# Regrouping a convolution tile and moving its layer norm between attention rounds in a two-block float32 forward pass

## The chip, the cores and the metric

The kernel runs on one core of a Trainium2 chip. The metric is device time in microseconds (us) of one execution of the whole program, as the median of several runs; lower is better. Five engines work side by side, each through its own instruction list in order, and they meet only at semaphores: TensorE (PE in the profile, with its weight loads as PEld), VectorE (DVE), ScalarE (ACT), GpSimd (POOL) and SyncE (SP), which here only issues transfers.

## The reference, cut to what matters

Two transformer blocks run one after the other on 512 tokens of width 1024. The change touches the middle of the second block only, which is this (`B, S = 1, 512`, eight heads of 64, 512 convolution channels, 31 taps):

```python
def _conformer_conv(val, gate, conv_w, conv_b, ln_g, ln_b):
    glu = val * jax.nn.sigmoid(gate)
    padded = jnp.pad(glu, ((0, 0), (CONV_WIDTH - 1, 0), (0, 0)))
    y = depthwise_conv(padded, conv_w) + conv_b            # 31 taps, 512 channels
    return jax.nn.silu(_layernorm(y, ln_g, ln_b))          # over the 512 channels

def second_block(...):
    u = _rmsnorm(h, g_pre_mix) @ w_in                      # val, gate, q, k, v
    conv_out = _conformer_conv(c_val, c_gate, conv_w, conv_b, conv_ln_g, conv_ln_b)
    # A[t,s] = sigmoid(z_ts) * prod_{s<j<t} (1 - sigmoid(z_tj)), s < t, per head
    attn_out = _rmsnorm(_stick_breaking(q, k, v), attn_norm_g)     # norm over each head's 64
    y = concat([conv_out, attn_out]) @ w_out               # the output product
    h = h + _rmsnorm(y, g_post_mix)
    # then a gated feed-forward part of width 2816 and a last residual
```

## The kernel before, in words

Every float32 product is made of three TensorE matmuls (`mm3`, lines 745 to 747): operands are split into a high part (fp32r) and a rest, and high by high, high by low and low by high are summed. Weights come in slabs of 128 x 1024; ScalarE makes the high part (`weights`, line 1375), VectorE the low part (line 1853).

The second block keeps channels on the partitions and the 512 tokens along the free axis. Channels 0 to 383 of the convolution (tiles 0 to 2) are done tap by tap on VectorE (`taps`, line 2264, 93 taps in all). Tile 3 is done on TensorE into PSUM bank 7: each tap is a product with a diagonal 128 x 128 matrix, whose high and low parts (`DH`, `DL`, 16 places) GpSimd makes in one instruction each for a run of taps (line 721). `CV_GROUPS` says which taps form a group; a group is one accumulation in bank 7, and its result is then copied or added into `CV[:, 3]` (`co`).

`PLAN_C` is a hand-written list of steps that all four engines walk in the same order; each engine issues only its part of a step. It has eight rounds, one for each head `u`:

- `lg u`: logits on TensorE (line 1158 and `mm3`), then Abs, Exp and Ln on ScalarE (lines 1706, 1708, 1710)
- `sp u`, `sl u`: softplus on VectorE (line 2314), its split (ScalarE line 1715, VectorE line 2318)
- `bt u-1`: the suffix sums on TensorE (line 1173); `ex u-1`: Exp of them (line 1721); `ah`/`at`: the split of the weights (lines 1727, 2322)
- `va u-2`: the product with the values, into bank 6; `kp`: its copy, and for odd heads the square (lines 1733, 1737)
- `ps`, `pr`, `pt`, `pl`: the norm of a pair of heads: sums by TensorE (line 1226) with a first VectorE step (line 1859), rsqrt and copy (line 1745), transposes into bank 7 (line 1231) with the multiplication (line 2337), and the split into the output product's input `M2h`/`M2l` (lines 1751, 2341)
- one step of `BEHIND`: in rounds 0 to 3 an input tile (q2, k2, q3, k3), in rounds 4 to 6 a convolution group, in round 7 the layer norm's sums `ln_sub`

The layer norm of the convolution is: `ln_sub` (sum over channels on TensorE, line 1239; subtraction on VectorE, line 2345; squares on ScalarE, line 1757), `ln_var` (sums of the squares, 32 matmuls of two columns, line 1245), `ln_rs` (rsqrt), `ln_mul` (transposes, line 1251; multiplication, line 2354), then for each tile `silu` (lines 1763, 1766) and `ll` (line 2358).

After the eight rounds stands a tail with the last heads, the rest of the norms and the first strips of the output product. `OUT_KS` says which two 128-row parts of the mixed input a slab of `w_out` covers: rows 0 to 3 are the convolution tiles, rows 4 to 7 the head pairs. `OUT` is the order of the eight slabs (column half n, slab j); a slab is four strips (128 tokens each) of six matmuls into bank 4n + t. Banks 0 to 2 and 3 to 5 carry the logits of even and odd heads, bank 6 the values, bank 7 everything in `IN_7`, each of whose steps waits until the one before has been read.

Of the kernel before, what the change touches and what calls it, by code (L numbers as in the profile page):

```python
# [98 lines left out]
def build(nc, cols, ins, out):  # L99
    sems = {}  # L100

    def S(name):
        if name not in sems:
            sems[name] = nc.alloc_semaphore(f"s_{name}")
        return sems[name]
# [63 lines left out]
    SL, CH = {}, {}  # L169
# [62 lines left out]
    for x in IN_LATER:  # L232
        in_tile(x)

    OUT_KS = [[4, 5], [6, 7], [0, 1], [2, 3]]
    OUT = [(0, 0), (0, 1), (0, 2), (1, 0), (1, 1), (1, 2), (0, 3), (1, 3)]
    for n, j in OUT:
        SL["out", n, j] = slab([(W["w_out_2"][0], 512 * n, 512)], 128 * OUT_KS[j][0], 2)
# [136 lines left out]

    CV_GROUPS = [range(0, 10), range(10, 20), range(20, 31)]
    TAPS = [(j, k) for j in range(3) for k in range(31)]
    PLAN_C = []  # L380
    for n, x in enumerate(IN_FIRST):
# [1 line left out]
    for j in range(4):  # L383
        PLAN_C += [("v2", j), ("w", CH["v2"].first + min(j, 2) + 3), ("taps", 4)]
    PLAN_C += [("v2_out",)]
    BEHIND = [("tile", x) for x in IN_LATER] + [("cv", g) for g in range(3)] + [("ln_sub",)]
    for u in range(8):
        b = BEHIND[u - 1] if u else ("", "")
        if b[0] == "tile":
            PLAN_C += [("ev", b[1])]  # L390
        elif b[0] == "cv":
            PLAN_C += [("co", b[1])]
        PLAN_C += [("lg", u), ("taps", 2)]
        if u >= 4:
            PLAN_C += [("pt" if u % 2 else "ps", u // 2 - 2)]
        PLAN_C += [("taps", 2)]
        if u >= 1:
            PLAN_C += [("bt", u - 1)]
        if u >= 2:
            PLAN_C += [("va", u - 2)]  # L400
        PLAN_C += [("sp", u)]
        if u >= 1:
            PLAN_C += [("ex", u - 1)]
        if b[0] == "tile":
            PLAN_C += [("lo", b[1])]
        if u >= 4 and u % 2 == 0:
            PLAN_C += [("pr", u // 2 - 2)]
        PLAN_C += [("sl", u)]
        if u >= 1:
            PLAN_C += [("ah", u - 1), ("at", u - 1)]  # L410
        if u >= 2:
            PLAN_C += [("kp", u - 2)]
        PLAN_C += [BEHIND[u]]
        if u < 5:
            PLAN_C += [("w", CH["v2"].last + min(u, 3) + 4)]
        if u >= 4 and u % 2:
            PLAN_C += [("pl", u // 2 - 2)]
        PLAN_C += [("taps", 2 if u < 6 else 100)]
    PLAN_C += [("bt", 7), ("ps", 2), ("va", 6), ("ex", 7), ("pr", 2), ("o", (0, 1, 2)), ("ah", 7), ("at", 7), ("kp", 6),
               ("ln_var",), ("pt", 2), ("ln_rs",), ("va", 7), ("kp", 7), ("pl", 2), ("ps", 3), ("pr", 3), ("ln_mul",),  # L420
               ("o", (3,)), ("pt", 3), ("silu", 0), ("pl", 3)]
    for j in range(1, 4):
        PLAN_C += [("silu", j), ("ll", j - 1)]
    PLAN_C += [("ll", 3)]

    PAIR_SUMS = {4: 1, 2: 0, 6: 2}
    EV = [s[1] for s in PLAN_C if s[0] == "tile" and s[1][0] != "v"]
# [214 lines left out]
    def gpsimd_program(e):  # L642
# [59 lines left out]
        for step in PLAN_C:  # L702
            if step[0] == "tile" and step[1][0] == "g":
                j = GATES.index(step[1])
                q.wait_ge(S("sig"), j + 1)
                TTT(T4[:, j % 2, :], T4[:, j % 2, :], RB[:, :], ALU.mult).then_inc(S("sig_r"), 1)
            elif step[0] == "cv":

                taps = CV_GROUPS[step[1]]
                for part in ([k for k in taps if k < 16], [k for k in taps if k >= 16]):  # L710
                    if not part:
                        continue
                    n, k0 = len(part), part[0] % 16
                    q.wait_ge(S("w_used"), SL["in", "k3"] + 1)
                    q.wait_ge(S("cw"), 2)
                    if part[0] >= 16:
                        q.wait_ge(S("cv_used"), 1 + (part[-1] >= 26))
                    eye = IDENT.unsqueeze(1).broadcast_to([128, n, 128])
                    at = slice(part[0], part[-1] + 1)
                    for dst, w in ((DH, CWH[:, at].bitcast(F32)), (DL, CWL[:, at])):  # L720
                        TTT(dst[:, k0:k0 + n, :], eye, w.unsqueeze(2).broadcast_to([128, n, 128]), ALU.mult).then_inc(
                            S("diag"), 1)
# [9 lines left out]
    def tensor_program(e):  # L732
# [456 lines left out]
        def conv_group(g):  # L1189
            taps = CV_GROUPS[g]  # L1190
            q.wait_ge(S("cv_g"), 1)
            for k in taps:
                q.wait_ge(S("diag"), 8 if g == 2 else 6 if k >= 16 else 2 * g + 2)
                x = slice(k, k + T)
                m = mm3(banks[7][:, :], DH[:, k % 16, :], DL[:, k % 16, :], GLH[:, x], GLL[:, x], k == taps[0],
                        k == taps[-1])
            m.then_inc(S("cv_used"), 1)

        def block_step(kind, *a):
            step = (kind,) + a  # L1200
            if step in IN_7:
                free_7(step)
            if kind == "tile":
                n = IN_FIRST.index(a[0]) if a[0] in IN_FIRST else -1
                tile_t(Ah, Al, "pre_mix", n % 4 if n >= 0 else 7, lambda: in_free(n) if n >= 0 else None,
                       turn_in_tile(X, "pre_mix") if n == 0 else no_step)
                if n == 0:
                    q.wait_ge(S("turn_lo"), 8 * JOB["pre_mix"] + 8)
                    spread(X, "pre_mix")
            elif kind == "v2":  # L1210
                v2_slab(a[0])
            elif kind == "lg":
                logits(a[0])
            elif kind == "bt":
                between(a[0])
            elif kind == "va":
                values(a[0])
            elif kind == "cv":
                conv_group(a[0])
            elif kind == "o":  # L1220
                out_first(a[0])
            elif kind == "ps":
                q.wait_ge(S("pair_sq"), a[0] + 1)
                q.wait_ge(S("keep"), 2 * a[0] + 2)
                for t in range(4):
                    m = mm(banks[6][:, 2 * t:2 * t + 2], OQ[:, 128 * t:128 * t + 128], HALF[:, :], start=True, stop=True)
                m.then_inc(S("pair_ps"), 1)
            elif kind == "pt":
                q.wait_ge(S("pair_b"), a[0] + 1)
                for t in range(4):  # L1230
                    m = e.transpose(banks[7][:, 128 * t:128 * t + 128], TN[:, 128 * t:128 * t + 128], IDENT)
                m.then_inc(S("pair_t"), 1)
            elif kind == "ln_sub":
                for j in range(4):
                    if j == 3:
                        q.wait_ge(S("cv_ev"), len(CV_GROUPS))
                    else:
                        q.wait_ge(S("tap"), 31 * j + 31)
                    m = mm(banks[7][:, :], ONES, CV[:, j, :], start=j == 0, stop=j == 3)
                m.then_inc(S("ln_ps"), 1)  # L1240
            elif kind == "ln_var":
                for t in range(4):
                    for j in range(4):
                        q.wait_ge(S("ln_act"), j + 1)
                        m = mm(banks[7][:, 2 * t:2 * t + 2], GL[:, j, 128 * t:128 * t + 128], ONES[:, 0:2], start=j == 0,
                               stop=j == 3)
                m.then_inc(S("ln_ps"), 1)
            elif kind == "ln_mul":
                q.wait_ge(S("rs_n"), 3 * USE["ln",] + 3)
                for t in range(4):  # L1250
                    m = e.transpose(banks[7][:, 128 * t:128 * t + 128], LNR[:, t:t + 1].broadcast_to([128, 128]), IDENT)
                m.then_inc(S("ln_ps"), 1)
# [18 lines left out]
        def out_strip(w, j, n, t):  # L1271
            return strip(w, OUT_KS[j], t, 4 * n + t, M2h, M2l, mixed_ready, j == 0, j == 3)

        def out_first(tiles):
# [4 lines left out]
            for t in tiles:  # L1279
                q.wait_ge(S("sb_exp"), 21 if t < 3 else 24)  # L1280
                m = out_strip(held, 0, 0, t)
                if t == 3:
                    m.then_inc(S("w_used"), 1)

        def last_strips(order, step, done):

            w = []
# [10 lines left out]
        held.clear()  # L1298
        for step in PLAN_C:
            block_step(*step)  # L1300
        q.wait_ge(S("pair_n"), 4)
        q.wait_ge(S("keep"), 8)
        for n, j in OUT[1:5]:
            w = next_slab()
            for t in range(4):
                m = out_strip(w, j, n, t)
            m.then_inc(S("w_used"), 1)
        last_strips(OUT[5:], out_strip, "o_tile")


# [47 lines left out]
    def scalar_program(e):  # L1358
# [316 lines left out]
        def block_step(kind, *a):  # L1675
# [71 lines left out]
            elif kind == "pl":  # L1747
# [1 line left out]
                q.wait_ge(S("pair_n"), p + 1)  # L1749
                q.wait_ge(S("w_used"), SL["in", "k3"] + 1)  # L1750
                act(M2h[:, 4 + p, :], TN, ACT.Copy).then_inc(S("pair_hi"), 1)
            elif kind == "ln_sub":
                q.wait_ge(S("tap"), len(TAPS))
                q.wait_ge(S("cv_g"), 1)
                for j in range(4):
# [81 lines left out]
    def vector_program(e):  # L1837
# [450 lines left out]
        def block_step(kind, *a):  # L2288
# [49 lines left out]
            elif kind == "pl":  # L2338
                p = a[0]
                q.wait_ge(S("pair_hi"), p + 1)  # L2340
                tt(M2l[:, 4 + p, :], TN, M2h[:, 4 + p, :].bitcast(F32), ALU.subtract).then_inc(S("pair_lo"), 1)
            elif kind == "ln_sub":
                q.wait_ge(S("ln_ps"), 1)
                for j in range(4):
                    stt(CV[:, j, :], banks[7][:, :], -1.0 / 512, CV[:, j, :], ALU.mult, ALU.add).then_inc(S("ln_dve"), 1)
# [153 lines left out]
```

## Time and profile before

| what | value |
|---|---|
| median of 3 runs | 1868.67 us (1867.34 to 1868.72) |
| the profiled execution's own time | 1870.3 us |
| span of its trace (first to last instruction) | 1868.5 us |
| mean granted TensorE clock | 0.986 |
| PE busy | 1812.6 us, 97% |
| DVE, ACT, POOL busy | 953.3, 751.7, 127.4 us |
| chain that ended last | PE 86%, DVE 10%, ACT 3% |

A time "in the trace" is counted from the first instruction of the span. In the timeline view, instructions of one line that follow each other are merged into a row with their count; a bracket at the end of a row is how long the engine stood idle before it and which instruction released it. The stretch that the change touches lies between 1350 and 1487 us.

### The profile page before, as it was taken

Reading aid. Unit: us, or ns where it says so; the run is one execution under the profiler, and the core shown is the slowest. Engines: PE = TensorE matmul, PEld = TensorE weight load, DVE = VectorE, ACT = ScalarE, POOL = GpSimd, SP = SyncE. Lnnn points to the kernel's source line nnn. Section 1 sums busy time; section 2 is a strip of 40 time slices with the busy share of each in tenths; the row PEclk is TensorE's granted clock in tenths of the full one; section 3 lists DMA queues with packets and bytes.
Section 4 is the critical chain, followed back from the end, with each engine's and each line's share of the span. In section 5 each row is a group of like instructions: output and inputs, shape, how many; then the busy total and the mean of one; then the engine's idle time right before and its main releaser. Section 6 shows DMA issues by size and latency. Waiting matters only on the chain.

```text
span 1868.5 us, 21601 instructions
## 1 busy us (share of the span) xinstructions
PE 1812.6 (97%) x8477; PEld 1482.4 (79%) x8477; DVE 953.3 (51%) x1702; ACT 751.7 (40%) x1475; POOL 127.4 (7%) x163
## 2 busy tenths in 40 slices
PE   8999999999999999999999999998998999999997
PEld 7887888888887777777888888786777788888886
DVE  5666443434345666755344434489954544243345
ACT  7333432323235565644232323423765543232233
POOL 0000010101001111001010101010020000000000
PEclk9999999999999999999999999999998999999999
DMA  7222233333332111112333333232100333333331
GB/s 246 81 69 90 72 109 90 102 94 99 101 95 80 57 57 57 35 57 81 100 99 95 98 95 99 79 91 68 46 11 1 91 101 102 100 92 102 91 101 56
DMA packets 195748, 158.37 MB, mean 85 GB/s; under 512 B 5248, under 2 KB 161152, under 8 KB 195648
## 3 DMA queue, kind: packets, MB, share of 16 engines
q1 hardware_dynamic: 194240, 154.16, 27.4%
q0 software_dynamic: 400, 1.25, 0.3%
q8 instruction: 67, 1.10, 0.2%
q10 hardware_dynamic: 1008, 1.59, 0.2%
q14 instruction: 33, 0.27, 0.0%
HBM read 154.88 MB, written 2.10 MB: 84 GB/s over the span
## 4 chain that ended last, share of the span: by engine, by line
PE 86%; DVE 10%; ACT 3%; issue 1%; DMA 0%; SPq 0%; DVEq 0%; ACTq 0%
PE ps L745 28%; PE ps L747 27%; PE ps L746 27%; DVE sb L2264 3%; DVE sb L1853 1%; PE ps L797 1%; PE ps L1173 1%; PE ps L1061 0%; DVE sb L2388 0%; DVE sb L1879 0%; PE ps L1067 0%; DVE sb L1851 0%; PE ps L856 0%; PE ps L1037 0%; DMA sb<-in_mem 0%
## 5 line engine op out<-in xcount | busy, mean ns | idle before, releaser
L745 PE MATMUL ps<-sb,sb 128*128 128x512 f32 (+3 forms) x2547 | 991.1, 391 | 16.9 <-DVE sb L1859 5.5
L747 PE MATMUL ps<-sb,sb 128*128 128x512 f32 (+3 forms) x2547 | 968.2, 382 | 0.0
L746 PE MATMUL ps<-sb,sb 128*128 128x512 f32 (+3 forms) x2547 | 968.1, 382 | 0.0
L745 PEld LDWEIGHTS ps<-sb,sb 128*128 128x128 f32 (+1 forms) x2547 | 479.8, 189 | 125.8 <-issue 19.7
L747 PEld LDWEIGHTS ps<-sb,sb 128*128 128x128 f32 (+1 forms) x2547 | 479.5, 189 | 93.0
L746 PEld LDWEIGHTS ps<-sb,sb 128*128 128x128 f32 (+1 forms) x2547 | 480.6, 190 | 86.0
L1853 DVE TENSOR_TENSOR sb<-sb,sb 128x512 fp32r<-128x512 f32 x532 | 351.4, 700 | 347.2 <-ACT sb L1375 346.3
L1375 ACT ACTIVATE sb<-sb 128x512 fp32r<-128x512 f32 x532 | 305.5, 622 | 428.4 <-PE ps L747 427.1
L2068 DVE TENSOR_TENSOR sb<-sb,sb 128x512 fp32r<-128x512 f32 x64 | 68.0, 1063 | 176.9 <-ACT sb L1524 176.9
L1534 ACT ACTIVATE sb<-ps 128x512 f32<-128x512 f32 x64 | 38.4, 599 | 208.6 <-PE ps L747 208.6
L651 POOL TENSOR_TENSOR sb<-sb 128x512 f32<-128x512 f32 x64 | 66.9, 1045 | 786.6 <-ACT sb L1534 786.6
L2264 DVE SCALAR_TENSOR_TENSOR sb<-sb,sb,sb 128x512 f32<-128x512 f32 x90 | 74.0, 823 | 2.4
L2048 DVE SCALAR_TENSOR_TENSOR sb<-ps,sb,sb 128x512 f32<-128x512 f32 x64 | 47.9, 749 | 18.9 <-PE ps L747 18.3
L2431 DVE TENSOR_TENSOR sb<-ps,sb 128x512 f32<-128x512 f32 x22 | 15.2, 692 | 72.1 <-PE ps L747 71.6
L1810 ACT ACTIVATE sb<-sb 128x512 f32<-128x512 f32 x22 | 13.9, 633 | 93.8 <-DVE sb L2431 93.8
L797 PE MATMUL ps<-sb,sb 128*128 128x128 f32 x176 | 28.2, 299 | 15.0 <-DVE sb L1879 5.4
L1524 ACT ACTIVATE sb<-sb 128x512 fp32r<-128x512 f32 x64 | 39.9, 624 | 5.1 <-POOL sb L651 5.1
L1879 DVE SCALAR_TENSOR_TENSOR sb<-ps,sb,sb 128x512 fp32r<-128x512 f32 (+1 forms) x48 | 31.4, 701 | 18.9 <-ACT sb L1394 18.9
L2438 DVE TENSOR_TENSOR sb<-ps,sb 128x512 f32<-128x512 f32 x22 | 15.2, 692 | 48.0 <-PE ps L747 48.0
L797 PEld LDWEIGHTS ps<-sb,sb 128*128 128x128 f32 x176 | 22.5, 152 | 20.9 <-DMA sb<-in_con 5.2
L1851 DVE SCALAR_TENSOR_TENSOR sb<-sb,sb,sb 128x512 fp32r<-128x512 f32 x40 | 29.5, 748 | 17.8 <-ACT sb L1375 17.6
L1394 ACT ACTIVATE sb<-ps,sb 128x512 fp32r<-128x512 f32 (+1 forms) x48 | 28.5, 656 | 11.8 <-PE ps L797 11.7
(203 smaller groups left out, 1000.8 us busy)
## 6 DMA issues: line engine op xcount, KB each, us to landing
sb<-in_w_up SPq DMA_DIRECT2D x86, 512.0 KB, 4.0
sb<-in_w_down SPq DMA_DIRECT2D x86, 512.0 KB, 3.8
sb<-in_w_gate SPq DMA_DIRECT2D x22, 512.0 KB, 3.8
sb<-in_a_w_in SPq DMA_DIRECT2D x20, 512.0 KB, 3.9
sb<-in_w_in SPq DMA_DIRECT2D x20, 512.0 KB, 3.7
sb<-in_w_o SPq DMA_DIRECT2D x16, 512.0 KB, 3.8
sb<-in_w_mem_kv SPq DMA_DIRECT2D x8, 512.0 KB, 7.7
sb<-in_w_out SPq DMA_DIRECT2D x8, 512.0 KB, 3.8
```

What stands on the lines that cost most here:

```text
L651: TTT(T2[:, z, :], T1[:, z, :], T1[:, z, :], ALU.mult).then_inc(S("relu2"), 1)
L745: mm(ps, lh, rh, start=start, stop=False, **k)
L746: mm(ps, lh, rl, start=False, stop=False, **k)
L747: return mm(ps, ll, rh, start=False, stop=stop, **k)
L797: i = e.transpose(banks[4 + k % 4][:, 128 * t:128 * t + 128], src[:, t, 128 * k:128 * k + 128], IDENT)
L1375: act(WH[i % N_SPLIT][:, a], RAW[i % N_RAW][:, a], ACT.Copy, scale=g).then_inc(S("w_hi"), 1)
L1524: act(Bh[:, m % 8, :], T2[:, m % 2, :], ACT.Copy).then_inc(S("h_hi"), 1)
L1534: act(T1[:, m % 2, :], banks[m % 4][:, :], ACT.Relu).then_inc(S("relu"), 1)
L1853: tt(lo, raw, hi, ALU.subtract).then_inc(S("w_lo"), 1)
L2048: stt(x, ps, rms2(job, t, 1), x, ALU.mult, ALU.add).then_inc(S("res"), 1)
L2068: tt(Bl[:, m % 8, :], T2[:, m % 2, :], Bh[:, m % 8, :].bitcast(F32), ALU.subtract).then_inc(S("h_lo"), 1)
L2264: stt(CV[:, j, :], GL[:, j, k:k + T], col("convw", 4 * k + j), CV[:, j, :], ALU.mult, ALU.add).then_inc(S("tap"), 1)
```

## The change

Three things, all in the second block. The convolution tile on TensorE is done in two groups of 16 and 15 taps in place of three of 10, 10 and 11, so that its layer norm's `ln_sub` stands in round 6 instead of round 7; the subtraction (`ln_dv`, VectorE) and the squares (`ln_sq`, ScalarE) become steps of their own in round 7. The tail begins with `ln_var`, ahead of `bt 7`, and `ln_mul` and the `silu` steps come ahead of the third pair's norm. The rows of the output product are taken as 4-5, 0-1, 2-3, 6-7, and two slabs, (0,1) and (0,2), are multiplied (`os`) between the steps of the last pair's norm; the wait for the last pair's norm and for the last `kp` stands only where banks 6 and 7 are needed.

```diff
-    OUT_KS = [[4, 5], [6, 7], [0, 1], [2, 3]]
+    OUT_KS = [[4, 5], [0, 1], [2, 3], [6, 7]]
...
-    CV_GROUPS = [range(0, 10), range(10, 20), range(20, 31)]
+    CV_GROUPS = [range(0, 16), range(16, 31)]
...
-    BEHIND = [("tile", x) for x in IN_LATER] + [("cv", g) for g in range(3)] + [("ln_sub",)]
+    BEHIND = [("tile", x) for x in IN_LATER] + [("cv", g) for g in range(2)] + [("ln_sub",), ("none",)]
...
         PLAN_C += [("lg", u), ("taps", 2)]
+        if u == 7:
+            PLAN_C += [("ln_dv",)]
         if u >= 4:
             PLAN_C += [("pt" if u % 2 else "ps", u // 2 - 2)]
...
             PLAN_C += [("ah", u - 1), ("at", u - 1)]
+        if u == 7:
+            PLAN_C += [("ln_sq",)]
         if u >= 2:
             PLAN_C += [("kp", u - 2)]
...
-    PLAN_C += [("bt", 7), ("ps", 2), ("va", 6), ("ex", 7), ("pr", 2), ("o", (0, 1, 2)), ("ah", 7), ("at", 7), ("kp", 6),
-               ("ln_var",), ("pt", 2), ("ln_rs",), ("va", 7), ("kp", 7), ("pl", 2), ("ps", 3), ("pr", 3), ("ln_mul",),
-               ("o", (3,)), ("pt", 3), ("silu", 0), ("pl", 3)]
+    PLAN_C += [("ln_var",), ("bt", 7), ("ps", 2), ("ln_rs",), ("va", 6), ("ex", 7), ("pr", 2), ("o", (0, 1, 2)), ("ah", 7),
+               ("at", 7), ("kp", 6), ("ln_mul",), ("va", 7), ("silu", 0)]
     for j in range(1, 4):
         PLAN_C += [("silu", j), ("ll", j - 1)]
-    PLAN_C += [("ll", 3)]
+    PLAN_C += [("pt", 2), ("ll", 3), ("pl", 2), ("o", (3,)), ("kp", 7), ("w", SL["out", 0, 0] + 4), ("os", 0, 1), ("ps", 3),
+               ("pr", 3), ("w", SL["out", 0, 0] + 5), ("os", 0, 2), ("pt", 3), ("pl", 3)]
...
-                        q.wait_ge(S("cv_used"), 1 + (part[-1] >= 26))
+                        q.wait_ge(S("cv_used"), 1)
...
-                q.wait_ge(S("diag"), 8 if g == 2 else 6 if k >= 16 else 2 * g + 2)
+                q.wait_ge(S("diag"), 2 * g + 2)
...
+        def out_slab(n, j):
+            w = next_slab()
+            for t in range(4):
+                if (n, t) == (1, 2):
+
+                    q.wait_ge(S("pair_n"), 4)
+                    q.wait_ge(S("keep"), 8)
+                m = out_strip(w, j, n, t)
+            m.then_inc(S("w_used"), 1)
...
-        q.wait_ge(S("pair_n"), 4)
-        q.wait_ge(S("keep"), 8)
-        for n, j in OUT[1:5]:
-            w = next_slab()
-            for t in range(4):
-                m = out_strip(w, j, n, t)
-            m.then_inc(S("w_used"), 1)
+        for n, j in OUT[3:5]:
+            out_slab(n, j)
         last_strips(OUT[5:], out_strip, "o_tile")
```

## Rows read from the trace of the kernel before

**Rows 1.** The page: engine totals; the chain that ended last, by engine.
```profile
PE 1812.6 (97%) x8477; PEld 1482.4 (79%) x8477; DVE 953.3 (51%) x1702; ACT 751.7 (40%) x1475; POOL 127.4 (7%) x163
...
PE 86%; DVE 10%; ACT 3%; issue 1%; DMA 0%; SPq 0%; DVEq 0%; ACTq 0%
```

**Rows 2.** Timeline of PE, 1360 to 1424 us: start, length, what.
```profile
1360.88 0.76 PE L745 MATMUL ps<-sb,sb 128*128 128x512 f32 x1 [3.34 <-DVE sb L1859]
...
1372.62 0.50 PE L745 MATMUL ps<-sb,sb 64*128 64x512 f32 x1
...
1376.29 3.06 PE L1173 MATMUL ps<-sb,sb 128*128 128x256 f32 x20
1379.19 0.40 PE L745 MATMUL ps<-sb,sb 128*128 128x512 f32 x1
...
1381.14 0.40 PE L745 MATMUL ps<-sb,sb 128*128 128x512 f32 x1
...
1388.20 0.50 PE L745 MATMUL ps<-sb,sb 64*128 64x512 f32 x1
...
1404.99 0.49 PE L745 MATMUL ps<-sb,sb 64*128 64x512 f32 x1
...
1413.51 3.60 PE L1239 MATMUL ps<-sb,sb 128*128 128x512 f32 x8
...
1416.54 3.39 PE L1173 MATMUL ps<-sb,sb 128*128 128x256 f32 x20
...
1422.84 0.48 PE L745 MATMUL ps<-sb,sb 128*128 128x512 f32 x1 [2.13 <-DVE sb L1859]
```

**Rows 3.** Timeline of DVE in round 4: a tap beside GpSimd, one alone.
```profile
1353.30 2.81 DVE L2264 SCALAR_TENSOR_TENSOR sb<-sb,sb,sb 128x512 f32<-128x512 f32 x1
...
1360.58 0.16 DVE L1859 TENSOR_SCALAR sb<-ps 128x8 f32<-128x8 f32 x1
1360.69 0.75 DVE L2264 SCALAR_TENSOR_TENSOR sb<-sb,sb,sb 128x512 f32<-128x512 f32 x1
```

**Rows 4.** Timeline of POOL: the first diagonal instruction alone, and the first four.
```profile
1350.48 2.34 POOL L721 TENSOR_TENSOR sb<-sb,sb 128x1280 fp32r<-128x1280 f32 x1 [101.56 <-PE ps L747]
...
1350.48 8.84 POOL L721 TENSOR_TENSOR sb<-sb,sb 128x1280 fp32r<-128x1280 f32 x4 [101.56 <-PE ps L747]
```

**Rows 5.** Windows: busy us (count) of PE, PEld, DVE, ACT, POOL; clock; DMA.
```profile
1361.00:1367.00 6.00, 6.00 (x19) 5.18 (x20) 3.97 (x9) 2.99 (x4) 0.00 (x0) 0.52 0.00 0
...
1446.00:1451.00 5.00, 4.62 (x11) 3.38 (x12) 3.01 (x5) 4.54 (x7) 0.00 (x0) 0.50 0.00 0
```

**Rows 6.** Timelines of DVE and ACT: rounds 6 and 7.
```profile
1401.42 1.62 DVE L2322 TENSOR_TENSOR sb<-sb,sb 128x1408 fp32r<-128x1408 f32 x1
...
1418.24 2.48 DVE L2345 SCALAR_TENSOR_TENSOR sb<-ps,sb 128x512 f32<-128x512 f32 x4
...
1411.84 1.45 ACT L1721 ACTIVATE sb<-ps 128x512 f32<-128x512 f32 x3
1413.75 1.38 ACT L1715 ACTIVATE sb<-sb 128x1408 fp32r<-128x1408 f32 x1 [0.46 <-DVE sb L2314]
...
1419.04 2.34 ACT L1757 ACTIVATE sb<-sb 128x512 f32<-128x512 f32 x4 [1.36 <-DVE sb L2345]
```

**Rows 7.** Timeline of PE: the tail (1245 twice: up to 1431.6, and whole).
```profile
1428.98 2.92 PE L1245 MATMUL ps<-sb,sb 128*128 128x2 f32 x25
...
1428.98 4.41 PE L1245 MATMUL ps<-sb,sb 128*128 128x2 f32 x32
...
1439.62 1.05 PE L1226 MATMUL ps<-sb,sb 128*128 128x2 f32 x8 [1.34 <-ACT sb L1737]
...
1444.42 1.11 PE L1231 MATMUL ps<-sb,sb 128*128 128x128 f32 x4 [1.39 <-DVE sb L2354]
1446.38 0.79 PE L745 MATMUL ps<-sb,sb 128*128 128x512 f32 x1 [0.85 <-DVE sb L2337]
...
1487.30 0.38 PE L797 MATMUL ps<-sb,sb 128*128 128x128 f32 x2
```

More of the change, by code:

```diff
@@ L1221, in block_step @@
                 out_first(a[0])
+            elif kind == "os":
+                out_slab(*a)
             elif kind == "ps":
@@ L1751, in block_step @@
                 act(M2h[:, 4 + p, :], TN, ACT.Copy).then_inc(S("pair_hi"), 1)
-            elif kind == "ln_sub":
+            elif kind == "ln_sq":
                 q.wait_ge(S("tap"), len(TAPS))
@@ L2341, in block_step @@
                 tt(M2l[:, 4 + p, :], TN, M2h[:, 4 + p, :].bitcast(F32), ALU.subtract).then_inc(S("pair_lo"), 1)
-            elif kind == "ln_sub":
+            elif kind == "ln_dv":
                 q.wait_ge(S("ln_ps"), 1)
```

## The prediction, made before the change was run

> **What bounds the kernel now.** I read the page first. TensorE is busy for 97% of the span and carries 86% of the chain that ended last [rows 1], so the change is worth what it takes out of TensorE's stops and out of its time at half clock; the matmuls themselves stay the same (31 taps, eight slabs). Then I read TensorE's timeline from round 4 to the end of the output product. It stops once in round 4, for 3.34 us [rows 2], and in the tail for 2.13 [rows 2], 1.34, 1.39 and 0.85 us [rows 7], plus 0.26 us after `ln_var`. The windows show the second cost: behind these stops the granted clock is 0.52 and 0.50 [rows 5], that is 1.2 GHz in place of 2.4. The product ends at 1487.30 [rows 7]. What follows (post norm, feed-forward) is untouched, so the change in that end is the change in the time.
>
> **Round 4, the longer diagonals.** GpSimd's first four diagonal instructions (1280, 1280, 768, 768 columns) take 8.84 us from 1350.48, 2.34 for the first [rows 4], that is 1.83 ns a column. Beside them a VectorE tap takes 2.81 us in place of 0.75 [rows 3]: VectorE gets one instruction with two SBUF inputs in between two of GpSimd's. The new group makes the same 4096 columns in two instructions of 2048, 3.75 us each. So VectorE gets through two fewer, 1.5 us of work, while GpSimd ends some 0.4 earlier and has two fewer turns to wait for. Written out from the rows: first VectorE instruction until 1354.7, GpSimd's second until 1358.4, VectorE's first tap until 1358.9, then one tap, one eviction, two taps: line 1859 (`ps 0`) starts at 1361.85 in place of 1360.58 [rows 3]. TensorE's `va 2` waits for it: +1.27 us. It starts at half clock as before [rows 5], and if that stretch ends at the same time, less work falls in it, which gives back 0.6: **+0.65**. Bounds: -0.1, if VectorE loses only time in proportion to GpSimd's columns, and +1.3, if nothing is given back. I take the middle, because the one row on a blocked tap shows a whole wait.
> The Trainium skill (SBUF — State Buffer, Who interferes with whom) says that a VectorE instruction with two SBUF inputs contends with GpSimd's reads, and that the one that issued first holds the shared ports for its whole instruction. By that rule this term is the +0.65; by a mere sharing in proportion it would be -0.1. The tap of 2.81 us agrees with the rule.
>
> **Rounds 4 to 6, moved taps.** Ten taps took 1381.14 to 1388.20 [rows 2], 0.706 each. Six more in round 4 and five more in round 5 are eleven fewer in round 6: 0. The second group's diagonals (2 x 1920 columns, 7.0 us) may start only when the first group is used. Their cover is `lg 5`, `pt 0`, `bt 4` and `va 3`, 1372.62 to 1381.14, 8.52 us [rows 2]; 1.4 us remain, so 0. If VectorE took two turns in between (0.45 us each in round 4) 0.5 would still remain. Rounds 5 and 6 start at 1377.5 and 1396.6. Round 6 is now 8.52 + 0.48 (sums in place of transposes) + 3.03 for `ln_sub` (1413.51 to 1416.54 [rows 2]), so round 7 starts at 1408.65 with `ln_sub` behind it, in place of 1404.99: 3.66 later, 3.03 of it moved.
>
> **Round 7, two new stops.** From here I count from its start. VectorE is free of `at 5` 14.8 us after round 6's start (1401.42 + 1.6 against 1388.20 [rows 6, 2]), at +2.7. The subtraction `ln_dv`, four instructions, takes 2.48 [rows 6] and ends at +5.2. `pt 1` shares bank 7 and waits for it, while TensorE is done with `lg 7` at +3.3: a stop of **1.9**. What is queued behind is `bt 6` (2.90, 1376.29 to 1379.19 [rows 2]) and `va 5` (1.95): they end at +8.55 and +10.5. ScalarE waits for `bt 6` with `ex 6` (ready at +6.9 before [rows 6]); then `ex 6` 1.35, `sl 7` and `ah 6` 1.3 each, and four squares 2.34 [rows 6] end at about +15.1. `ln_var` is the next step on TensorE and reads all four squares: a stop of **4.0**, after which 13 of its 16 products remain. In the old order `bt 7` would have stood here.
>
> **After `bt 7`.** Counted from its end: `ps 2` and the wait for line 1859 0.5, `va 6`, three strips, `ln_mul`, `va 7`; then `pt 2` waits 0.9 for the four multiplications (2.48), strip 3, slab (0,1) at +12.3 just as the second `ll` is done, `ps 3`, 0.55 until the split of slab (0,2)'s weights (ScalarE must first do `silu`, a table load, `pl 2` and `kp 7`), slab, `pt 3`, and 20 strips of 1.36 (a slab of 24 matmuls of 0.227). The last pair's norm lies under slabs (0,2) and (1,0), 10.9 us of cover for some 8. Sum 52.3. The weight transfers have room (DMA for each slab is issued a slab ahead), and the gain row `GP` is loaded about 10 us later but used only after the product.
>
> **Sum.** Before, from 1404.99 to 1487.30: 82.3 us = 68.3 of work at full clock, 6.9 of stops (5.97 and their latencies), 7.1 for half clock. After: 65.3 of work, stops 1.9 + 4.0 + 0.5 + 0.9 + 0.55 = 7.9. The clock: behind the stop of 4.0 comes `ln_var`, 25 of whose 32 matmuls took 2.92 us [rows 7], after which the clock was at 0.50. I expect half clock from `ln_var` until the end of `bt 7`, some 11.5 us, which costs 5.8. Round 7 starts 3.66 later, so the end moves by 3.66 + (65.3 + 7.9 + 5.8) - 82.3 = **+0.35**. Bounds of the clock term: if it recovers in the middle of `bt 7`, 2.3 less; if it also falls at the stop before `pt 1`, 0.7 more. So -2.0 to +1.05 with the middle at -0.5. The profiled execution took 1870.3 for its span of 1868.5, 1.6 over the median, but the sum is a difference, so it goes on the median: 1868.67 - 0.5 = **1868.2**. The five stops of the tail are gone, but about as long stops come before `ln_var` and `pt 1`. A measurement of this kernel tells about 0.2% (3.7 us) from no change.
>
> **Rivals.**
> (A) The forecast, no change that can be told: 1866.0 to 1870.3; 0.55.
> (B) The clock hardly falls. If the new stops cost no half clock at all, 5.8 goes: -5.4, 1863.3. For: after 2.13 us of stop at 1422.84 it stayed high [rows 2]. Against: after 3.34 it did not [rows 2, 5], and tiny matmuls were followed by 0.50. With a partial fall -4. Faster; 0.25.
> (C) Slower, by one mechanism: half clock goes on past `bt 7`. In the tail it held over 1446 to 1451 with TensorE 92% busy [rows 5]. If it lasts from the stop of 4.0 until the end of the three strips, another 7.9 us of full-clock work costs double: +7.9, at most 1877; it decides from 3.4 us of such work on, 1872.4. Against: in round 4, 6 us of dense work at half clock ended it. 0.15.
> (D) The second group's diagonals are late, the change's regrouping making a new stop in round 5: with VectorE's two splits of 1.6 us in between they end 3.2 later, less the 1.4 in hand, +1.8: 1870.0. Against: no VectorE instruction with two SBUF inputs stood in that part of round 5. Same; 0.05.
>
> **How the numbers follow.** Faster is B, 0.25; same is A and D, 0.60; slower is C, 0.15. The range of 8 in 10 reaches from just under B's full price, 1863.0, to C's threshold, 1872.5; A's own range is given above.
>
> **What would show it.** Four POOL instructions of about 3.7 us in place of eight. Line 1859 of `ps 0` about 1.3 us later. No stop before the second group. `pt 1` waiting for `ln_dv` about 2 us; the first `ln_var` matmuls waiting for ScalarE's squares about 4 us; half clock over `ln_var` and `bt 7`; then no stop over 1 us until the product's end, at 1485.3 to 1488.4. Wrong would be: no half clock there, a long stop before (0,1) or (0,2) for `ll` or weights, or a late round 5.

## The result, and the profile after

The changed kernel took 1870.82 us in the median of 13 runs (1869.21 to 1874.96), the kernel before 1868.65 us in 13 runs beside it. The medians are 2.2 us apart. The ratio, which is not that of the medians, is 1.0017, that is 3.2 us, with a 95% interval of 1.0009 to 1.0025 (1.7 to 4.7 us). The change makes the kernel slower. Both figures are inside the 0.2% (3.7 us) that I called no change and inside the range, but I had forecast 0.5 us less, and the interval leaves out any gain. All medians here and below are of fast executions alone; one of e1's five, a slow one of 2519.93 us, is left out.

The page of the changed kernel hardly differs in its totals [rows 1]: engines, then the chain that ended last.

```profile
PE 1813.0 (97%) x8477; PEld 1484.8 (79%) x8477; DVE 952.5 (51%) x1701; ACT 751.1 (40%) x1475; POOL 126.0 (7%) x159
...
PE 86%; DVE 10%; ACT 3%; issue 1%; DMA 0%; SPq 0%; ACTq 0%; DVEq 0%
```

The profiled execution's span is 1868.5 us in both: this one reached round 4 0.79 us earlier (`lg 4` begins at 1349.54 against 1350.33) and took 0.77 us less behind the output product, outside the stretch that the change touches. So I measure from `lg 4`: from the first matmul of `lg 4` to the first transpose behind the output product it is 136.97 us before (1487.30 - 1350.33) and 138.53 after (1488.07 - 1349.54), 1.56 more. This is one execution of each kernel; the medians and the ratio say somewhat more, and no profile shows where the rest goes. Below, "stretch" means this length, and "the fall" the granted clock's going from 2.4 to 1.2 GHz.

TensorE's timeline after, to be laid beside [rows 2] and [rows 7]. Lines have moved: 749 to 751 are `mm3`, 1177 `bt`, 1237 `pt`, 1245 `ln_sub`, 1251 `ln_var`, 1864 the weights' low part, 1870 the first step of a norm.

```profile
1360.94 0.77 PE L749 MATMUL ps<-sb,sb 128*128 128x512 f32 x1 [4.20 <-DVE sb L1870]
...
1376.44 0.49 PE L749 MATMUL ps<-sb,sb 64*128 64x512 f32 x1
...
1380.53 4.20 PE L1177 MATMUL ps<-sb,sb 128*128 128x256 f32 x20
1384.57 0.40 PE L749 MATMUL ps<-sb,sb 128*128 128x512 f32 x1
...
1397.12 0.50 PE L749 MATMUL ps<-sb,sb 64*128 64x512 f32 x1
...
1406.10 3.60 PE L1245 MATMUL ps<-sb,sb 128*128 128x512 f32 x8
1409.63 0.50 PE L749 MATMUL ps<-sb,sb 64*128 64x512 f32 x1
...
1414.38 1.11 PE L1237 MATMUL ps<-sb,sb 128*128 128x128 f32 x4 [1.28 <-DVE sb L2356]
1415.15 3.99 PE L1177 MATMUL ps<-sb,sb 128*128 128x256 f32 x20
...
1423.89 7.17 PE L1251 MATMUL ps<-sb,sb 128*128 128x2 f32 x32 [2.83 <-ACT sb L1768]
1430.93 4.55 PE L1177 MATMUL ps<-sb,sb 128*128 128x256 f32 x20
1435.32 0.95 PE L1232 MATMUL ps<-sb,sb 128*128 128x2 f32 x8
1436.62 0.47 PE L749 MATMUL ps<-sb,sb 128*128 128x512 f32 x1 [0.35 <-DVE sb L1870]
...
1445.91 0.66 PE L1237 MATMUL ps<-sb,sb 128*128 128x128 f32 x4 [0.65 <-DVE sb L2365]
...
1454.82 0.50 PE L749 MATMUL ps<-sb,sb 128*128 128x512 f32 x1 [0.64 <-DVE sb L1864]
...
1488.07 0.38 PE L801 MATMUL ps<-sb,sb 128*128 128x128 f32 x2
```

The tail is what the change promises: behind `ln_var` no stop is longer than 0.65 us, where there were five up to 2.13. In their place stand the 1.28 us before `pt 1` (for the norm's subtraction) and the 2.83 us before `ln_var` (for the squares), and the 4.20 us in round 4. `ln_var` took 7.04 us to the next start, for matmuls that took 4.41 before, and `bt 4`, behind which and ahead of which TensorE did not stop, 4.04 us where it took 2.90. The windows say why (busy us of PE, PEld, DVE, ACT, POOL; clock; DMA): 1.2 GHz in rows at 0.50. The stop before `pt 1` is followed by half clock too, and `bt 6` behind it took 3.82 us (1415.15 to 1418.97) in place of 2.90.

```profile
1366.00:1376.40 10.40, 10.40 (x46) 8.20 (x44) 3.16 (x2) 1.93 (x3) 0.00 (x0) 1.00 0.00 0
1376.40:1379.60 3.20, 3.20 (x16) 2.06 (x15) 0.00 (x0) 1.78 (x3) 3.00 (x1) 1.00 0.02 5
1379.60:1383.00 3.40, 3.40 (x15) 3.28 (x15) 0.75 (x1) 2.88 (x3) 3.40 (x2) 0.50 0.00 0
...
1413.90:1417.00 3.10, 2.62 (x11) 2.62 (x12) 1.59 (x3) 2.62 (x2) 0.00 (x0) 0.50 0.00 0
1424.00:1434.00 10.00, 10.00 (x44) 9.82 (x45) 2.01 (x3) 3.46 (x8) 0.00 (x0) 0.50 0.00 0
```

Round 4 beside GpSimd, VectorE's timeline: one tap is held for 4.10 us, against 2.81 [rows 3]; line 1870's instruction for `ps 0` starts 11.10 us after `lg 4` (1360.64 - 1349.54), 0.85 later than before (1360.58 - 1350.33).

```profile
1353.79 4.10 DVE L2275 SCALAR_TENSOR_TENSOR sb<-sb,sb,sb 128x512 f32<-128x512 f32 x1
...
1360.64 0.16 DVE L1870 TENSOR_SCALAR sb<-ps 128x8 f32<-128x8 f32 x1
```

### The profile page after: what moved, and what is told of

Same layout as the page of the kernel before. It is cut to its first block, busy times and chain, and to the rows that moved or that the text cites. A ratio compares the mean times of both kernels' runs of the same rounds, so it can differ in the third digit from the quotient of the medians.

```text
span 1868.5 us, 21593 instructions
## 1 busy us (share of the span) xinstructions
PE 1813.0 (97%) x8477; PEld 1484.8 (79%) x8477; DVE 952.5 (51%) x1701; ACT 751.1 (40%) x1475; POOL 126.0 (7%) x159
## 4 chain that ended last, share of the span: by engine, by line
PE 86%; DVE 10%; ACT 3%; issue 1%; DMA 0%; SPq 0%; ACTq 0%; DVEq 0%
PE ps L749 28%; PE ps L751 27%; PE ps L750 27%; DVE sb L2275 3%; DVE sb L1864 1%; PE ps L1177 1%; PE ps L801 1%; PE ps L1251 0%; PE ps L1065 0%; DVE sb L2399 0%; DVE sb L1890 0%; PE ps L1071 0%; DVE sb L1862 0%; PE ps L860 0%; PE ps L1041 0%
```

## The experiments

Thirteen kernels, each timed against the kernel before on the same chip. Lines in the diffs are against the changed kernel or the kernel before, as said. The table gives medians, the ratio with its interval, and the stretch in each one's profile. In the text, gains and losses are differences of the medians; by the ratios they come out up to 1.4 us otherwise (e7: 5.7 us by the medians, 7.1 by the ratio).

| kernel | its median, before beside it | ratio (95%) | stretch |
|---|---|---|---|
| before | | 1 | 136.97 |
| changed | 1870.82, 1868.65 | 1.0017 (1.0009 to 1.0025) | 138.53 |
| e1 norm only | 1882.28, 1868.78 | 1.0071 (1.0058 to 1.0084) | 148.98 |
| e2 var behind | 1868.17, 1868.78 | 1.0001 (0.9993 to 1.0010) | 136.56 |
| e3 pool four | 1870.00, 1868.78 | 1.0004 (0.9994 to 1.0014) | 138.36 |
| e4 groups 15, 16 | 1869.86, 1868.78 | 1.0009 (1.0000 to 1.0018) | 138.36 |
| e5 fill | 1864.97, 1868.79 | 0.9976 (0.9966 to 0.9987) | 133.37 |
| e6 squares later | 1865.15, 1868.79 | 0.9983 (0.9972 to 0.9994) | 133.79 |
| e7 pt and var | 1863.09, 1868.79 | 0.9962 (0.9949 to 0.9975) | 131.08 |
| e8 fill, squares | 1862.18, 1868.79 | 0.9958 (0.9943 to 0.9973) | 130.35 |
| e9 pt alone | 1868.78, 1869.38 | 0.9997 (0.9989 to 1.0006) | 137.47 |
| e10 taps late | 1865.43, 1869.38 | 0.9975 (0.9965 to 0.9985) | 133.91 |
| e11 pt, var, taps | 1858.11, 1869.38 | 0.9936 (0.9924 to 0.9949) | 129.22 |
| e12 fill, squares, taps | 1856.21, 1869.38 | 0.9929 (0.9916 to 0.9941) | 124.23 |
| e13 two groups alone | 1872.19, 1868.99 | 1.0022 (1.0013 to 1.0032) | 142.19 |

**e1, the third part undone.** Changed kernel without the slabs between the last heads' steps:

```diff
-    OUT_KS = [[4, 5], [0, 1], [2, 3], [6, 7]]
+    OUT_KS = [[4, 5], [6, 7], [0, 1], [2, 3]]
...
-               ... ("kp", 7), ("w", SL["out", 0, 0] + 4), ("os", 0, 1), ("ps", 3), ("pr", 3), ("w", ...), ("os", 0, 2), ...]
+               ... ("kp", 7), ("ps", 3), ("pr", 3), ("pt", 3), ("pl", 3)]
...
-        for n, j in OUT[3:5]:
+        q.wait_ge(S("pair_n"), 4)
+        q.wait_ge(S("keep"), 8)
+        for n, j in OUT[1:5]:
```

> The changed kernel without its third part: rows of the output product in the old order (4-5, 6-7, 0-1, 2-3) and the four slabs behind all norm steps, with the wait for the last pair's norm ahead of them. My account (the slabs between the steps cover the last pair's norm, which the norm's new place pushes behind the four silu steps): TensorE stops about 5 us before ps 3 (ScalarE has silu, a table load, pl 2 and kp 7 first) and 3 us more around pt 3, with half clock behind it: 8 to 13 us over the changed kernel, 1879 to 1884. Rival (the slabs cover little, the loss of 2 us is theirs): within 2 us of the kernel before.

13.5 us over the kernel before, 11.3 over the changed kernel (the difference of the two differences), as my account said. Its timeline shows the stops that the slabs cover:

```profile
1448.10 1.87 PE L1231 MATMUL ps<-sb,sb 128*128 128x2 f32 x8 [5.01 <-ACT sb L1749]
1452.06 1.09 PE L1236 MATMUL ps<-sb,sb 128*128 128x128 f32 x4 [2.10 <-ACT sb L1757]
1453.99 0.80 PE L748 MATMUL ps<-sb,sb 128*128 128x512 f32 x1 [0.84 <-DVE sb L2349]
```

So the regrouping and the norm's earlier place, as ordered here, are dear, and the slabs pay for most of it.

**e2, `ln_var` behind `bt 7`.** Against the changed kernel:

```diff
-    PLAN_C += [("ln_var",), ("bt", 7), ("ps", 2), ("ln_rs",), ...
+    PLAN_C += [("bt", 7), ("ln_var",), ("ps", 2), ("ln_rs",), ...
```

> The changed kernel with ln_var behind bt 7 instead of ahead of it. My account (the changed kernel loses in round 7, where the moved ln_sub leaves a hole before bt 7 and ln_var waits for the squares): bt 7 starts about 2 us before ln_var did, covers the squares, and the stretch at 1.2 GHz over ln_var and bt 7 gets shorter: 2 to 4 us under the changed kernel, 1867 to 1869. Rival (the hole is there whichever step comes first, since bt 7 waits for the split of the softplus): within 1 us of the changed kernel.

Level with the kernel before, 2.8 us under the changed one (the differences to the kernel before beside each: -0.6 and +2.2). `bt 7` now waits 0.95 us and covers the squares; `ln_var` follows without a stop. The step that stands first begins 12.62 us after `lg 7` in place of 14.26, not quite the 2 us that I expected:

```profile
1415.79 0.96 PE L1237 MATMUL ps<-sb,sb 128*128 128x128 f32 x4 [1.23 <-DVE sb L2356]
...
1423.70 3.34 PE L1177 MATMUL ps<-sb,sb 128*128 128x256 f32 x20 [0.95 <-ACT sb L1726]
1426.88 4.29 PE L1251 MATMUL ps<-sb,sb 128*128 128x2 f32 x32
```

**e3 and e4, what lies behind round 4.** e3 makes the first group's diagonals in four GpSimd instructions, e4 takes groups of 15 and 16:

```diff
-                for part in ([k for k in taps if k < 16], [k for k in taps if k >= 16]):
+                for part in ([k for k in taps if k < 10], [k for k in taps if 10 <= k < 16], [k for k in taps if k >= 16]):
```
```diff
-    CV_GROUPS = [range(0, 16), range(16, 31)]
+    CV_GROUPS = [range(0, 15), range(15, 31)]
```

(In both, TensorE's waits for the diagonals are cut to the new instructions.)

> The changed kernel with the first group's diagonals in four GpSimd instructions (1280, 1280, 768, 768 columns) as in the kernel before, in place of two of 2048. My account: line 1859's instruction for ps 0 comes 0.8 to 1.3 us earlier, va 2 as in the kernel before (10.55 us after lg 4 in place of 11.40), and the total falls by 0.4 to 0.9 us. Rival (GpSimd's instruction length does not matter): va 2 stays at 11.4 and the total the same.

> The changed kernel with groups of 15 and 16 taps, so that round 5 begins 0.7 us earlier. The changed kernel ran bt 4 at 1.2 GHz (4.04 us in place of 2.90) though TensorE had not stopped since va 2; just before stood lg 5, whose matmuls use 64 rows. Theory 1 (where lg 5 falls in time decides): bt 4 takes 2.9 again and the total falls by 1 to 1.5 us. Theory 2 (a full stretch of taps, or GpSimd beside TensorE, brings the clock down): bt 4 still takes about 4 us and the total stays.

In e3 `va 2` came 10.54 us after `lg 4` (1360.23 - 1349.69), as in the kernel before: that part held. The total did not follow. `bt 4` was back at 3.08 us in both, but then `bt 5`, in round 6, ran at half clock instead, and the stretch is 138.36 in both. This is e3's round 6:

```profile
1399.38 4.61 PE L1177 MATMUL ps<-sb,sb 128*128 128x256 f32 x20
```

A full-clock `bt 4` speaks against theory 2. Theory 1's gain did not come in the stretch: the fall came in the next round. That the position of `lg 5` decides over `bt 4` is not shown. In e1 and e2, whose rounds 4 to 6 are the changed kernel's own, `bt 4` ran at full clock as well, and there the fall had come in round 4 (below, under what stays open). The medians (1870.00 and 1869.86) lie under the changed kernel's by 0.9 to 1.1 us against the kernel before beside them, with overlapping intervals; that is no verdict.

**e5 and e6, the kernel before with its tail repaired.** e5 keeps the old groups and the norm where it was and uses the other row order so that a slab of rows 4-5 of the right half can be a filler:

```diff
-    OUT_KS = [[4, 5], [6, 7], [0, 1], [2, 3]]
-    OUT = [(0, 0), (0, 1), (0, 2), (1, 0), (1, 1), (1, 2), (0, 3), (1, 3)]
+    OUT_KS = [[4, 5], [0, 1], [2, 3], [6, 7]]
+    OUT = [(0, 0), (1, 0), (0, 1), (0, 2), (1, 1), (1, 2), (0, 3), (1, 3)]
...
-               ("ln_var",), ("pt", 2), ("ln_rs",), ("va", 7), ("kp", 7), ("pl", 2), ("ps", 3), ("pr", 3), ("ln_mul",),
-               ("o", (3,)), ("pt", 3), ("silu", 0), ("pl", 3)]
+               ("ln_var",), ("w", SL["out", 0, 0] + 3), ("pt", 2), ("ln_rs",), ("va", 7), ("kp", 7), ("pl", 2), ("ln_mul",),
+               ("o", (3,)), ("ps", 3), ("pr", 3), ("oh", (0, 1)), ("pt", 3), ("oh", (2, 3)), ("silu", 0)]
...
```

(`oh` multiplies strips of slab (1,0); `pl 3` goes behind `silu 3`.) e6 splits `ln_sub` so that VectorE's and ScalarE's parts stand behind `pl 1` and `ps 2`:

```diff
-    PLAN_C += [("bt", 7), ("ps", 2), ("va", 6), ("ex", 7), ("pr", 2), ("o", (0, 1, 2)), ("ah", 7), ("at", 7), ("kp", 6),
-               ("ln_var",), ...
+    PLAN_C += [("bt", 7), ("ps", 2), ("va", 6), ("ex", 7), ("pr", 2), ("ln_dv",), ("o", (0, 1, 2)), ("ah", 7), ("at", 7), ("kp", 6),
+               ("ln_sq",), ("ln_var",), ...
```

> The kernel before (three groups, the layer norm's sums in round 7's hole) with only the idea of the third part: rows of the output product as 4-5, 0-1, 2-3, 6-7, and the second slab, rows 4-5 of the right half, multiplied between the last pair's norm steps, ln_mul ahead of ps 3. My account (the tail's last stops can be filled without moving the norm; moving it is what costs): the stops of 1.34, 1.39 and 0.85 us go, and with them most of the half clock behind them (4 us): 4 to 7 us under the kernel before, 1862 to 1865. Rival (the stops come back as a wait for silu and the split of the weights): within 2 us of it.

> The kernel before, with the norm's subtraction and squares queued behind the second pair's split and ps 2 instead of ahead of them; nothing else. In the kernel before, TensorE's stop of 2.13 us before va 6 waits for line 1859's instruction, which stands behind these on VectorE. My account: the stop falls to about 0.4 and the total by 1.5 to 2 us. Rival (the stop only moves to ln_var, which then waits for the squares): the total stays within 0.5 us.

e5 gained 3.8 us, just under what I expected: stops of 1.12, 0.84 and 1.32 us remained. e6 gained 3.6 (3.2 by its ratio, interval 1.1 to 5.2), about twice what the stop alone would give: the stop of 2.13 us before `va 6` became 0.35, and `ln_var` did not wait. It also ran at full clock, 3.63 us in place of 4.41. One moved pair of queue entries is worth more than the 0.5 us that I forecast for the whole change.

```profile
1420.13 0.47 PE L745 MATMUL ps<-sb,sb 128*128 128x512 f32 x1 [0.35 <-DVE sb L1859]
1426.25 3.63 PE L1245 MATMUL ps<-sb,sb 128*128 128x2 f32 x32
```

**e7 and e9, `pt 1` out of the norm's way.** Both put `pt 1` behind `va 5` and `sp 7`; e7 on top of e2, e9 with `ln_var` still ahead of `bt 7`:

```diff
-        if u >= 4:
+        if 4 <= u < 7:
             PLAN_C += [("pt" if u % 2 else "ps", u // 2 - 2)]
...
         PLAN_C += [("sp", u)]
+        if u == 7:
+            PLAN_C += [("pt", 1)]
```

> The changed kernel with ln_var behind bt 7 and pt 1 behind va 5 and sp 7, so that TensorE does not wait for ln_dv in round 7. My account: the stop of 1.3 us before pt 1 goes and ex 6 comes earlier, so that bt 7 starts 1.5 to 2.5 us earlier: 1.5 to 3 us under the run with ln_var alone behind bt 7, 1865.5 to 1867. Rival (bt 7 is bound by VectorE's and ScalarE's chain from lg 7 and the hole stays): less than 1 us.

> The changed kernel with pt 1 behind va 5 and sp 7, ln_var still ahead of bt 7: the fourth corner beside the changed kernel, ln_var alone behind bt 7 (-2.7 us), and both (-7.7). My account (pt 1's wait for ln_dv delays bt 6, ex 6 and with them the squares and bt 7, so it costs with either order): 3 to 5 us under the changed kernel, 1866 to 1868. Rival (with ln_var first the squares set the time, and pt 1's place is worth nothing): within 1 us of the changed kernel.

Against the kernel before: changed +2.2, `ln_var` behind -0.6, `pt 1` behind -0.6, both -5.7. Each repair is worth 2.8 us and both together 7.9; I had expected less of the pair and a little more of `pt 1` alone. The ratios (+3.2, +0.2, -0.6, -7.1) give the same picture. The profiles fit this reading: with `ln_var` first the earlier `bt 6` lengthens the wait for the squares (3.39 us in e9) and 7.04 us of `ln_var` at half clock still follow. In e7 only 1.51 us before `bt 7` is left, and `ln_var` runs at full clock, in half of the 7.17 us of the changed kernel. In e2, behind `bt 7` too, it took 4.29, so its place alone does not settle its clock:

```profile
1418.00 3.33 PE L1179 MATMUL ps<-sb,sb 128*128 128x256 f32 x20 [1.51 <-ACT sb L1728]
1421.16 3.63 PE L1253 MATMUL ps<-sb,sb 128*128 128x2 f32 x32
```

**e8, both repairs of the kernel before.** The edits of e5 and e6.

> The kernel before with both: the second slab's strips between the last pair's norm steps, and the norm's squares queued later. My account: the two gains add, 6 to 9 us under the kernel before, 1860 to 1863, and TensorE has no stop over 1 us from round 5 to the end of the product. Rival (the clock's stretches, not the stops, set the end): not more than 3 us under it.

-6.6 us against -3.8 and -3.6: nearly the sum. The second part of my account did not hold: a stop of 1.42 us and one of 1.33 remained.

**e10, the last taps late.** Against the changed kernel; five taps go from the end of round 3 and from round 4, ahead of `ps 0` and `sp 4`, to the end of round 4:

```diff
-        PLAN_C += [("lg", u), ("taps", 2)]
+        PLAN_C += [("lg", u), ("taps", 2 if u < 4 else 0)]
...
-        PLAN_C += [("taps", 2)]
+        PLAN_C += [("taps", 2 if u < 4 else 0)]
...
-        PLAN_C += [("taps", 2 if u < 6 else 100)]
+        PLAN_C += [("taps", 2 if u < 3 else 0 if u == 3 else 100)]
```

> The changed kernel with VectorE's last five taps behind everything of round 4 instead of ahead of ps 0 and sp 4, so that they neither stand beside GpSimd's diagonals nor ahead of line 1859's instruction. My account (TensorE's stop of 4.2 us before va 2 and the half clock behind it come from taps that GpSimd holds up): no stop before va 2, bt 3 to the first group at full clock, 5 to 7 us under the changed kernel, 1864 to 1866. Rival (VectorE's weight split is held up just the same, or the diagonals are late for the first group): less than 2 us.

6.1 us under the changed kernel, and no stop before `va 2`: `bt 3` started at 1352.28 and `va 2` at 1355.19. VectorE's weight split is still held up (its two instructions take 4.71 us), but the eviction from PSUM, 0.68 us, and line 1870's instruction pass beside GpSimd, whose second instruction runs until 1355.95 (1348.30 + 7.65):

```profile
1347.77 4.71 DVE L1864 TENSOR_TENSOR sb<-sb,sb 128x512 fp32r<-128x512 f32 x2
1352.40 0.68 DVE L2296 SCALAR_TENSOR_TENSOR sb<-ps,sb 128x512 f32<-128x512 f32 x1
1353.00 0.15 DVE L1870 TENSOR_SCALAR sb<-ps 128x8 f32<-128x8 f32 x1
```

**e11 and e12, everything together.** e11 is the changed kernel with the edits of e7 and e10, e12 the kernel before with those of e8 and e10.

> The changed kernel with all three repairs: pt 1 behind sp 7, ln_var behind bt 7, the last taps late. If the three are independent, 7.7 and 5 to 7 us add: 1857 to 1859. If the clock gives back only part, 1860 to 1862.

> The kernel before (three groups, the norm's sums in round 7) with the second slab as filler, the squares queued later, and the last taps late. If they are independent: 6.6 and 5 to 7 us under the kernel before, 1855 to 1857. Which of this and the repaired changed kernel is lower tells whether the two groups and the norm's earlier place are worth anything once the queues are in order: my account expects them within 2 us of each other, the rival expects the changed kernel's structure to be 3 us or more ahead.

e11 is 11.3 us under the kernel before, e12 13.2: both beat both kernels. They lie within 2 us, their intervals overlap, and the one without the change's regrouping is not behind. The late taps are worth 6.6 us in the kernel before as well (e12 against e8). With the queues in order, the norm's earlier place brings nothing that a filled tail does not.

**e13, the regrouping by itself.** Against the kernel before; with it go the two simpler waits of the change's diff:

```diff
-    CV_GROUPS = [range(0, 10), range(10, 20), range(20, 31)]
+    CV_GROUPS = [range(0, 16), range(16, 31)]
...
-    BEHIND = [("tile", x) for x in IN_LATER] + [("cv", g) for g in range(3)] + [("ln_sub",)]
+    BEHIND = [("tile", x) for x in IN_LATER] + [("cv", g) for g in range(2)] + [("none",), ("ln_sub",)]
```

> The kernel before with groups of 16 and 15 taps and nothing behind va 4 in round 6; the norm's sums stay in round 7, the tail and the output product as before. My account (the regrouping itself costs: a longer hold-up by GpSimd in round 4, and a round 6 of 8.9 us of TensorE work against about 13 us of ScalarE's, so that TensorE waits for bt 7 about 2 us): 2 to 5 us over the kernel before, 1871 to 1874, which is the price that ln_sub in round 6 and the new tail had to win back. Rival (the groups are neutral, and the changed kernel's loss is all in the norm's new order): within 1 us of the kernel before.

3.2 us slower, inside what I expected, but not by the mechanism: TensorE did not wait for `bt 7`. Round 6 is 9.07 us of TensorE work and ScalarE and VectorE are then behind, which shows later, at `va 6`:

```profile
1414.87 3.33 PE L1173 MATMUL ps<-sb,sb 128*128 128x256 f32 x20
...
1422.54 0.47 PE L745 MATMUL ps<-sb,sb 128*128 128x512 f32 x1 [3.54 <-DVE sb L1859]
...
1456.03 0.50 PE L745 MATMUL ps<-sb,sb 128*128 128x512 f32 x1 [1.60 <-DVE sb L1853]
```

The stop of 2.13 us has become 3.54, a wait of 1.60 for a weight split is new, and `va 2` comes 12.28 us after `lg 4` in place of 10.55, behind a `bt 3` at half clock. In this profile round 4 is 1.7 us longer than before (28.24 us for 22.29 and six taps), rounds 5 and 6 are as long as their work, and from `lg 7` to the end of the product it is 3.4 us more (85.75 for 82.31). These make the stretch's 5.2 us; the medians say 3.2, the ratio 4.1.

## Why the prediction was wrong, point by point

**Right in mechanism and near in size.** Line 1859's instruction in round 4: +0.85 for +1.27, and of the 0.65 that should reach round 5 0.37 did (1376.44 - 1349.54 against 1372.62 - 1350.33 and six taps). GpSimd's 2048 columns took 3.63 us for 3.75. The rule of the Trainium skill named in that step (SBUF — State Buffer, Who interferes with whom) is borne out by the tap of 4.10 us, beside a GpSimd instruction of 4.06. The second group was not late. The stop before `pt 1`: 1.28 for 1.9. The stop before `ln_var`: 2.83 for 4.0, in part because half clock on `pt 1` and `bt 6`, which the sum had only as a bound of 0.7, brought TensorE there 0.9 us later. Half clock over `ln_var` and `bt 7`: 1424.0 to about 1434, for 11.5 us. From the end of `bt 7` to the end of the product: 52.75 for 52.3, with stops of 0.35, 0.65 and 0.64. The last pair's norm was covered. From the start of round 7 to the end of `bt 7`: 25.69 for 26.7.

**The step that failed.** "Rounds 4 to 6, moved taps", put at 0. The count of the taps was right, the clock was not: I took 2.4 GHz from the first group to `pt 1`, because TensorE would have no stop there, and the clock fell without one. Round 5 took 20.68 us for 19.12, the excess being `bt 4` at half clock (4.04 for 2.90) and the transposes ahead of it. Round 6 took 12.51 for 12.05: `ln_sub` had been read as 3.03 us, from start to start, where 3.53 pass until `lg 7`. So round 7 began 60.09 us after `lg 4` and not 58.32; this 1.8, less the 1.0 won in round 7 and plus 0.45 behind it, makes the trace's +1.56 out of my sum of +0.35. It is not one execution's chance: from `lg 4` to `lg 7` my sum had 58.32 us, and the seven profiles with these rounds, exactly or nearly (changed, e1, e2, e3, e4, e7, e9), took 59.6 to 61.5. The step asked where TensorE would stop, and took the clock to be high wherever it did not. The kernel before had a row against that, in its first block: TensorE is busy throughout, its last stop of more than 0.2 us ended at 730.21, and the clock is at half speed in the second row (windows as above):

```profile
734.00:736.00 2.00, 2.00 (x13) 1.70 (x13) 1.25 (x4) 0.42 (x2) 0.00 (x0) 0.83 0.00 0
736.00:738.00 2.00, 2.00 (x6) 1.43 (x6) 1.84 (x3) 1.20 (x3) 0.00 (x0) 0.50 0.00 0
```

**The second fault was mine in the choosing.** The sum said +0.35, and I went to -0.5 as the middle of bounds that held only the clock's doubt in the tail. No bound of that kind stood on rounds 4 to 6, where the change moves TensorE's work as well. With it, the middle would have been on the slower side.

**The rivals.** B, no half clock, did not happen in the changed kernel. Its size was not tested: e7, with `ln_var` and `bt 7` at full clock, is 5.7 us faster than the kernel before where B had said 5.4, but e7's stops are shorter too, so the likeness of the two figures shows nothing. C, half clock far past `bt 7`, did not happen. D did not.

**What the change is worth, piece by piece.** Regrouping alone costs 3.2 us (e13). The norm's new order on top of it, with the output product as before, makes that 13.5 (e1). The slabs between the last heads' steps take 11.3 of it back, which leaves the changed kernel's 2.2. Two places in its queues cost 7.9: with both moved it is 5.7 under the kernel before (e7). I did foresee both of these stops, and priced them against what they replaced; what I did not ask is whether they had to be there.

**What stays open.** What makes the clock fall in rounds 4 to 6 while TensorE is busy. It came in the profiles of all ten kernels with two groups: in round 5 in the changed kernel, e7 and e9, in round 6 in e3, e4 and e10, in round 4, during `bt 3`, in e1 and e13, and in rounds 4 and 6 in e2 and e11. In rounds 4 to 6 of the five with three groups (before, e5, e6, e8, e12) it did not. Up to the end of `bt 3` TensorE's list is the same in both sorts, so four in ten against none in five is no proof for that place. The program of e1 and e9 is the same until `lg 7`. Here is e1's `bt 3`, with TensorE not stopping until it ends, then windows of e1 over the steps before it and a part of it, and over a part of round 5, and last e9's over the same part of round 5:

```profile
1350.25 4.61 PE L1176 MATMUL ps<-sb,sb 128*128 128x256 f32 x20
...
1346.20:1350.20 4.00, 4.00 (x24) 2.86 (x24) 4.00 (x2) 2.58 (x5) 3.93 (x2) 1.00 0.00 0
1350.20:1353.20 3.00, 3.00 (x16) 2.90 (x16) 3.00 (x2) 2.79 (x3) 3.00 (x1) 0.60 0.00 0
1374.00:1384.00 10.00, 10.00 (x60) 8.11 (x59) 2.50 (x4) 7.35 (x10) 6.76 (x2) 1.00 0.01 2
```
```profile
1374.00:1384.00 10.00, 10.00 (x51) 8.24 (x51) 2.51 (x4) 6.35 (x9) 6.76 (x2) 0.83 0.01 2
```

So the place of the fall differs from one execution to the next, and the time hardly does: from `lg 4` to `lg 7` e1 took 59.93 us, e9 60.21 and the changed kernel 60.09. GpSimd is not needed for it: it was idle in round 6 of e3 and in the first block's rows above. What stood just before the falls of the changed kernel, of e1 and of the first block is a run of logits, whose matmuls use 64 rows, with their bf16 matmuls of 128 columns; that these are the cause is an inference, no run changes them, and in the kernels with three groups `lg 4` to `lg 6` bring no fall. Since no kernel with two groups was without a fall, its price in the medians is not measured either; of the changed kernel's stretch it is some 1.5 us.

## What to carry to other kernels

When work is moved out of a hole in the critical engine's list, ask what fills the hole: here `ln_sub` left 3 us free ahead of `bt 7`, and the stops before `pt 1` and `ln_var` opened in its place. Before regrouping work, look in each in-order queue at what stands ahead of the instruction that the critical engine waits for: moving two entries of the kernel before (e6) gave 3.6 us, five taps out of GpSimd's way (e10) 6.1. A step of many tiny matmuls is better placed behind dense work than behind a stop: `ln_var` cost 7.04 us behind the stop, and behind `bt 7` 3.5 in e7 (1421.16 to 1424.65) and 4.15 in e2. And a sum should carry a bound for the clock also where the critical engine does not stop.

## What the runs showed of the hardware that was not expected

- The clock can fall to 1.2 GHz while TensorE is busy all the time: in the changed kernel's round 5 the row with 3.20 of 3.20 us busy is at 1.00 and the row behind it, with 3.40 of 3.40, at 0.50.
- VectorE and GpSimd took turns, one instruction each, as the prediction had it, so the length of GpSimd's instruction is the price of each VectorE instruction with two SBUF inputs beside it: 2.81 us beside 1280 columns, 4.10 beside 2048, for a tap of 0.75. What was not expected: an instruction that reads one of its operands from PSUM passed beside GpSimd at its usual 0.68 us (e10, 1352.40).
- A table load on ScalarE did not wait for the activation's data: in the changed kernel it ran 1440.77 to 1442.05, and the first `silu` behind it began at 1444.10, when VectorE's multiplication was done.

```profile
1440.77 1.28 ACT L1774 ACT_TABLE_LOAD   x1
1444.10 0.82 ACT L1774 ACTIVATE sb<-sb,sb 128x512 f32<-128x512 f32 x1 [2.05 <-DVE sb L2365]
```
